# Delta-rule inverse in packed 64x64 blocks, mask applied at the eviction, last level on one quarter

## What is computed

```python
def chunk_gated_delta_rule(q, k, v, g, beta):
    ...
    m = jnp.where(strict, jnp.einsum('bhncd,bhnsd->bhncs', k_beta, k) * decay, 0.0)
    rhs = jnp.concatenate([v_beta, k_beta * jnp.exp(g)[..., None]], axis=-1)
    sol = lax.linalg.triangular_solve(m + jnp.eye(C, dtype=jnp.float32), rhs, left_side=True, lower=True,
                                      unit_diagonal=True)
    u = sol[..., :Dv]
    w = sol[..., Dv:]
    intra = jnp.where(lower_incl, jnp.einsum('bhncd,bhnsd->bhncs', q, k) * decay, 0.0)
```

## Time and profile before

| | us |
|---|---|
| median of three runs | 2671.65 |
| their lowest and highest | 2669.71, 2673.22 |
| the profiled execution | 2668.37 |
| span of the profiled execution (first to last instruction) | 2666.6 |
| mean granted clock of TensorE | 0.992 of 2.4 GHz |
| TensorE busy | 2585.2 |
| loop of layer 0, L1178's first start to L1242's first | 63.1 |
| loop of layer 1, the same | 62.3 |

### The profile page before, as it was taken

One profiled execution on the slowest core, in us unless ns is written; L12 is line 12 of the kernel. 1 busy time (PEld: TensorE's weight loads), 2 busy tenths in 40 slices (PEclk: granted clock), 3 DMA queues, 4 the chain that ended last, 5 costly groups with the idle time before them and its releaser, 6 DMA issues.

```text
span 2666.6 us, 34482 instructions
## 1 busy us (share of the span) xinstructions
PE 2585.2 (97%) x11814; PEld 2057.1 (77%) x11814; DVE 1553.7 (58%) x1973; ACT 1122.2 (42%) x1610; POOL 112.4 (4%) x101
## 2 busy tenths in 40 slices
PE   7999999999999999999989899999899999899998
PEld 5768888887678888876679778888676788688886
DVE  4656755756556736656886554344569775543444
ACT  5554433435554424432565442232424754422323
POOL 1000000000000000000110010000102000100000
PEclk9999999999999999999999999999999999999998
DMA  4203332333113323342210223233222201233332
GB/s 131 72 1 95 95 110 87 100 101 87 33 42 98 108 84 95 104 110 63 57 56 1 64 79 106 85 100 100 66 64 56 64 9 48 71 98 99 95 98 91
DMA packets 394583, 208.01 MB, mean 78 GB/s; under 512 B 9738, under 2 KB 392660, under 8 KB 394484
## 3 DMA queue, kind: packets, MB, share of 16 engines
q1 hardware_dynamic: 391396, 202.79, 26.4%
...
## 4 chain that ended last, share of the span: by engine, by line
PE 89%; DVE 6%; ACT 3%; issue 1%; DMA 0%; SPq 0%; DVEq 0%; ACTq 0%
PE ps L607 64%; PE ps L626 6%; PE ps L884 2%; PE ps L1178 2%; PE ps L1192 1%; DVE ps L2693 1%; DVE x_sb L2696 1%; ACT whi L1402 1%; PE ps L1037 1%; PE ps L1052 1%; PE ps L1204 1%; DVE yc L2432 1%; DVE h_lo L2687 1%; PE ps L939 1%; PE ps L941 1%
## 5 line engine op out<-in xcount | busy, mean ns | idle before, releaser
L1402 ACT ACTIVATE whi<-raw 128x1024 fp32r<-128x1024 f32 (+1 forms) x354 | 395.8, 1119 | 1062.7 <-PE ps L607 946.3
L607 PE MATMUL ps<-h_hi,whi 128*128 128x512 f32 x1984 | 788.3, 397 | 4.6 <-ACT whi L1402 4.0
L607 PE MATMUL ps<-h_lo,whi 128*128 128x512 f32 x1984 | 772.8, 389 | 0.0
L607 PE MATMUL ps<-h_hi,wlo 128*128 128x512 f32 x1984 | 530.3, 389 | 0.0
L2030 DVE TENSOR_TENSOR wlo<-raw,whi 128x1024 fp32r<-128x1024 f32 (+1 forms) x354 | 458.6, 1296 | 55.5 <-ACT whi L1402 54.5
L607 PEld LDWEIGHTS ps<-h_hi,whi 128*128 128x128 f32 x1984 | 372.7, 188 | 89.6 <-ACT whi L1402 8.2
L607 PEld LDWEIGHTS ps<-h_lo,whi 128*128 128x128 f32 x1984 | 372.6, 188 | 82.5 <-issue 6.2
L607 PEld LDWEIGHTS ps<-h_hi,wlo 128*128 128x128 f32 x1984 | 372.4, 188 | 77.4
L607 PE MATMUL ps<-a_hi,whi 128*128 128x512 f32 x592 | 230.3, 389 | 0.0
L607 PE MATMUL ps<-a_lo,whi 128*128 128x512 f32 x592 | 230.3, 389 | 0.0
L2728 DVE TENSOR_TENSOR cv<-ps,rstd 128x512 f32<-128x512 f32 x88 | 60.9, 692 | 248.9 <-PE ps L607 241.0
...
## 6 DMA issues: line engine op xcount, KB each, us to landing
...
```

Of the source, the lines that this page charges most:

```text
L607: return pe.matmul(ps[:, ACC[s], :], w[s][:, k, :], r[:, k, :], start=start, stop=stop)
L1402: act.activation(whi[s][:, 0:kt, :], raw[s][:, 0:kt, :], ACT.Copy).then_inc(w_hi_ready.sem, 1)
```

## The change

Every matrix is 128x128 and, up to the next to last level, block diagonal with two 64x64 blocks. The change keeps only these blocks (`HB` = 64). `xd` and `xdT` (X and its transpose) each hold 4 x 64 columns, partitions 0 to 63 for the upper block and 64 to 127 for the lower, both inside `gk`. A product of one head becomes 8 of 64x64 with 64 columns: for each chunk one that reads and writes partitions 0 to 63, and one that reads and writes 64 to 127 of the same bank. Turning becomes a product with a 64x64 identity. The mask is applied to the first product when VectorE takes it from PSUM (`p1c`), in place of ScalarE's copy and of `lt`; `lev` holds turned masks for that. The second product goes to `ACC`, and the layer norm's sums to `TRN`. The update of n-1 stands in VectorE's iteration n. In steps 16 to 19 it writes the two blocks into `xT`, in two operations; the last level (steps 20 to 23) has 4 products of one quarter, ScalarE copies the first with its sign turned, and VectorE copies the second into the quarter of `xT` that is left. GpSimd zeroes columns 0 to 63 of each matrix of `xT` once per layer, behind head 0. In the heads, q k' comes before k k', turning uses bank `STAT[0]`, and the mask of level 0 is two operations on 64 partitions.

```diff
-        lt, p1, mrs2, msq2 = kb, dm, kb, sqt
+        p1, mrs2, msq2 = dm, kb, sqt
+        p1c = dm[:, 0, :].rearrange("p (a n) -> p a n", a=2)
+        xd, xdT = gk[:, :, 0:TB * HB], gk[:, :, TB * HB:2 * TB * HB]
...
                     delta_head(h)
+                    if h == 0:
+                        nc.gpsimd.memset(xT[:].rearrange("p h (t d) -> p (h t) d", d=P)[:, :, 0:HB], 0.0).then_inc(low_zeroed.sem, 1)
...
                 def head_products(h):
+                    if h >= 1:
+                        pe.wait_ge(intra_made.sem, intra_made.at(L, h - 1))
+                    for tb in range(TB):
+                        mm = pe.matmul(ps[:, STAT[1], tb * P:(tb + 1) * P], gk[:, h, tb * P:(tb + 1) * P],
+                                       gq[:, h, tb * P:(tb + 1) * P], start=True, stop=True)
+                    mm.then_inc(qk_ready.sem, 1)
                     pe.wait_ge(kb_ready.sem, kb_ready.at(L, h))
                     if h >= 1:
-                        pe.wait_ge(intra_made.sem, intra_made.at(L, h - 1))
+                        pe.wait_ge(x0_new.sem, x0_new.at(L, h - 1))
                     for tb in range(TB):
                         mm = pe.matmul(ps[:, STAT[0], tb * P:(tb + 1) * P], gk[:, h, tb * P:(tb + 1) * P],
                                        kb[:, h % 2, tb * P:(tb + 1) * P], start=True, stop=True)
                     mm.then_inc(kk_ready.sem, 1)
-                    if h >= 1:
-                        pe.wait_ge(x0_new.sem, x0_new.at(L, h - 1))
-                    for tb in range(TB):
-                        mm = pe.matmul(ps[:, STAT[1], tb * P:(tb + 1) * P], gk[:, h, tb * P:(tb + 1) * P],
-                                       gq[:, h, tb * P:(tb + 1) * P], start=True, stop=True)
-                    mm.then_inc(qk_ready.sem, 1)
...
                 def head_turned(h):
                     pe.wait_ge(lt0_ready.sem, lt0_ready.at(L, h))
                     for tb in range(TB):
-                        c = slice(tb * P, (tb + 1) * P)
-                        mm = pe.transpose(ps[:, STAT[1], c], xT[:, h, c], ident[:])
+                        for r in range(2):
+                            rows_r, c = block(r, tb, HB)
+                            mm = pe.matmul(ps[rows_r, STAT[0], c], xdT[rows_r, h, c], ident[rows_r, rows_r], start=True, stop=True)
                     mm.then_inc(p0_ready.sem, 1)
...
                 def level_first(n):
                     h = n % GH
-                    pe.wait_ge(lt_ready.sem, lt_ready.at(L, n))
                     if n == 0:
                         pe.wait_ge(eg_ready.sem, eg_ready.at(L, GH - 1))
                     elif n == 1:
                         pe.wait_ge(kb_ready.sem, kb_ready.at(L, GH - 1))
+                    elif n < STEPS - GH + 2:
+                        pe.wait_ge(p1_masked.sem, p1_masked.at(L, n - 2))
                     else:
-                        pe.wait_ge(p1_kept.sem, p1_kept.at(L, n - 2))
-                    if n >= GH:
+                        pe.wait_ge(p1_turned.sem, p1_turned.at(L, n - 2 - (STEPS - GH)))
+                    if n < GH:
+                        pe.wait_ge(x0_new.sem, x0_new.at(L, n))
+                    else:
                         pe.wait_ge(xt_kept.sem, xt_kept.at(L, n - GH))
                     for tb in range(TB):
-                        c = slice(tb * P, (tb + 1) * P)
-                        mm = pe.matmul(ps[:, ROT[n % 2], c], lt[:, n % 2, c], gk[:, h, c], start=True, stop=True)
+                        c = slice(tb * HB, (tb + 1) * HB)
+                        if n < STEPS - GH:
+                            for r in range(2):
+                                rows_r, diag_c = block(r, tb, P)
+                                mm = pe.matmul(ps[rows_r, ROT[n % 2], c], gv[rows_r, h, diag_c], xd[rows_r, h, c], start=True, stop=True)
+                        else:
+                            mm = pe.matmul(ps[HB:P, ROT[n % 2], c], gv[0:HB, h, tb * P + HB:(tb + 1) * P], xd[0:HB, h, c],
+                                           start=True, stop=True)
                     mm.then_inc(p1_ready.sem, 1)
...
                 def level_second(n):
                     h = n % GH
-                    pe.wait_ge(p1_kept.sem, p1_kept.at(L, n))
-                    if n < GH:
-                        pe.wait_ge(x0_new.sem, x0_new.at(L, n))
+                    if n < STEPS - GH:
+                        pe.wait_ge(p1_masked.sem, p1_masked.at(L, n))
+                    else:
+                        pe.wait_ge(p1_turned.sem, p1_turned.at(L, n - (STEPS - GH)))
                     if n >= 2:
                         pe.wait_ge(x_new.sem, x_new.at(L, n - 2))
                     else:
-                        pe.wait_ge(turned_used.sem, turned_used.at(L, GH - 1))
+                        pe.wait_ge(acc_free.sem, V * 2 + N_IN2 + 2)
                     for tb in range(TB):
-                        c = slice(tb * P, (tb + 1) * P)
-                        mm = pe.matmul(ps[:, TRN[n % 2], c], p1[:, n % 2, c], xT[:, h, c], start=True, stop=True)
+                        c = slice(tb * HB, (tb + 1) * HB)
+                        if n < STEPS - GH:
+                            for r in range(2):
+                                rows_r = slice(HB * r, HB * (r + 1))
+                                mm = pe.matmul(ps[rows_r, ACC[n % 2], c], p1c[rows_r, n % 2, c], xdT[rows_r, h, c], start=True, stop=True)
+                        else:
+                            mm = pe.matmul(ps[0:HB, ACC[n % 2], c], p1c[HB:P, n % 2, c], xT[HB:P, h, tb * P + HB:(tb + 1) * P],
+                                           start=True, stop=True)
                     mm.then_inc(xpt_ready.sem, 1)
...
+                        pe.wait_ge(intra_made.sem, intra_made.at(L, GH - 1))
                     for tb in range(TB):
-                        c = slice(tb * P, (tb + 1) * P)
-                        mm = pe.transpose(ps[:, STAT[n % 2], c], xT[:, h, c], ident[:])
+                        c = slice(tb * HB, (tb + 1) * HB)
+                        if n < STEPS - 2 * GH:
+                            for r in range(2):
+                                rows_r = slice(HB * r, HB * (r + 1))
+                                mm = pe.matmul(ps[rows_r, STAT[n % 2], c], xdT[rows_r, h, c], ident[rows_r, rows_r], start=True, stop=True)
...
+                    if n == 2:
                         head_turned(GH - 1)
                     if n == 15:
...
-                    act.wait_ge(p1_ready.sem, p1_ready.at(L, n))
-                    if n >= 2:
+                    if n >= STEPS - GH:
+                        act.wait_ge(p1_ready.sem, p1_ready.at(L, n))
                         act.wait_ge(xpt_ready.sem, xpt_ready.at(L, n - 2))
-                    else:
-                        act.wait_ge(intra_made.sem, intra_made.at(L, GH - 2 + n))
-                    order.told(act.activation(p1[:, n % 2, :], ps[:, ROT[n % 2], :], ACT.Copy), p1_kept, L, n)
+                        order.told(act.activation(p1c[HB:P, n % 2, :], ps[HB:P, ROT[n % 2], 0:TB * HB], ACT.Copy, scale=-1.0),
+                                   p1_turned, L, n - (STEPS - GH))
                     if 0 <= n - 2 < STEPS - GH:
+                        upto = P if n - 2 < STEPS - 2 * GH else HB
                         act.wait_ge(xt_turned.sem, xt_turned.at(L, n - 2))
-                        order.told(act.activation(gk[:, (n - 2) % GH, :], ps[:, STAT[n % 2], :], ACT.Copy), xt_kept, L, n - 2)
+                        order.told(act.activation(xd[0:upto, (n - 2) % GH, :], ps[0:upto, STAT[n % 2], 0:TB * HB], ACT.Copy), xt_kept, L, n - 2)
...
                     dve.wait_ge(turned_used.sem, turned_used.at(L, h))
-                    order.told(dve.tensor_tensor(intraT[:, h, :], ps[:, STAT[1], :], dm[:, s, :], ALU.mult), intra_made, L, h)
-                    order.settle()
-                    order.told(dve.tensor_tensor(by_token(xT[:, h, :]), by_token(gv[:, h, :]),
-                                                 lev[:, 0, :].unsqueeze(1).to_broadcast([P, TB, P]), ALU.mult), lt0_ready, L, h)
+                    order.told(dve.tensor_tensor(gv[:, h, :], ps[:, STAT[0], :], dm[:, s, :], ALU.mult), intra_made, L, h)
+                def head_masked(h):
+                    order.settle()
+                    for r in range(2):
+                        rows_r = slice(HB * r, HB * (r + 1))
+                        ins = dve.tensor_tensor(by_block(xdT[rows_r, h, :]), by_token(gv[rows_r, h, :])[:, :, rows_r],
+                                                lev[rows_r, 0, :].unsqueeze(1).to_broadcast([HB, TB, HB]), ALU.mult)
+                        if r == 0:
+                            order.step(ins)
+                        else:
+                            order.told(ins, lt0_ready, L, h)
...
                     order.settle()
-                    order.step(dve.tensor_tensor(by_token(gk[:, h, :]), unit_blocks, by_token(ps[:, STAT[1], :]), ALU.subtract))
```

(50 more changed lines are left out.)

35 lines of the change are left out of this document (22 added, 13 removed).

## The result

The changed kernel takes 2651.61 us (2649.48 to 2655.48), the kernel before on the same chip 2671.13 (2669.71 to 2673.22): a ratio of 0.9928, with a 95% interval of 0.9911 to 0.9945. The change takes off 19.5 us where I had forecast 33; 2651.6 lies in the range, 13.6 us above the predicted 2638. The profiled execution's span is 2648.6 us, 18.0 less than before, and TensorE's mean granted clock is 0.987 (0.992 before).

What follows compares the result with a forecast made beforehand. TensorE was taken to bound the kernel, with VectorE close behind. Gains of 1.0+3.0+2.3+6.3+4.1 = 16.7 us per layer, 33 for two, gave 2638 us; the range was 2626 to 2662, holding about 0.8.

Steps and rivals of the forecast that it cites:

- The pair of tiles: Two 64x64 matmuls in different array tiles run side by side at 0.058 us a pair, 0.46 us per product.
- the low bound: Pair pace taken from L823's second weight loads starting 0.06 us later, against 0.110 at the other bound; chance 0.60.
- The rule of the Trainium skill: Different row tiles cannot access the same PSUM bank simultaneously; by it the pair of tiles would serialize.
- doesn't go below 0.110: Rival: tiles take turns on the bank or the sequencer limits feeding; products 0.88 us, 2676 us, slower; chance 0.13.
- in between: Rival: feeding costs something, 0.080 us a pair, a step of 1.92, 2653 us; chance 0.18.
- signs of being wrong: A product taking 0.64 us or more, TensorE waiting in plain steps, or granted clock 0.50 beyond the entry.
- The heads: Heads before the loop: shorter VectorE operations and the query product filling a wait; about 1.0 us off per layer.
- The entry: From head 2's turning to the first L1204: 11.0 us instead of 14.06, 3.0 off per layer.
- Steps 3 to 7: Loop steps with a convolution tap, bounded by VectorE: 1.76 us instead of 2.22, 2.3 off per layer.
- The plain steps: Loop steps without a tap, bounded by TensorE: 1.39 us instead of 2.22; steps 8 to 15 give 6.3 off per layer.
- The end: From the first product of step 16 to L1242: 16.9 us instead of 21.0, 4.1 off per layer.
- the clock as a rival: Clock stays at 1.2 GHz through the loop, as small tiles with waits may not count as work; 2695 us; chance 0.06.

Runs made afterwards that it cites:

- late masks: The changed kernel, with GpSimd masking the four intraT only after the update of step 9 instead of behind each head: 2646.92 us, ratio 0.9911.
- All together with the taps: The changed kernel with GpSimd's masks late, taps in steps 4, 6, 8, 10, 12 and 13, and filler matmuls at loop end, heads and entry: 2640.03 us.
- second profile: The changed kernel run again, unedited, to stand beside the edited runs: 2650.72 us, ratio 0.9931.

## Why the forecast was right in sign and half right in size

**The pair of tiles** was right: 0.058 us forecast, 0.0583 measured, granted clock 1.00. The choice of the low bound by the weight loads of L823 held. The rule of the Trainium skill that the prediction names against it has no effect to be seen here: both row tiles write the same bank, on different partitions, and the pair does not serialize; where the page and this measurement differ, the measurement decides. The rival "doesn't go below 0.110" is out, and so is "in between".

**The number is partly luck.** The case that came true, the pair at 0.058, had its own range of 2628 to 2648, and the measured time is 3.6 us above it. It lies in the band given to "in between", 2648 to 2662, whose mechanism did not occur. The stated range held the time because it was wide enough for a rival that is out. One of the prediction's own signs of being wrong also came up: the granted clock was 0.50 beyond the entry, in the first products behind it, at the loop's end and in the right-hand sides. And the product that stands at L1242 came 12.3 us sooner after head 2's turning in layer 0 and 14.0 in layer 1, not some 16.

**The heads** were the first term that failed. I had 1.0 off; in layer 0, head 0's turning to head 2's went from 18.4 us (1368.57 to 1386.96) to 20.9 (1368.55 to 1389.46), 2.5 more. The step was "Splitting the mask in two adds 0.1": it added 1.17 (1.86 for 0.69), because GpSimd's mask runs in between. I had written of GpSimd that nobody needs its zeros before the loop ends, and not asked whether its operations hold up VectorE's. The halved subtractions did shrink by 0.53, as forecast. VectorE also stood 0.37 us longer ahead of them in layer 0 (0.47 for 0.10, in layer 1 not), which no run explains. With that, k k' of head 1 starts 0.86 later than q k' did (1372.69, 1371.83). The other 1.6 us is the clock: from there to the next weights takes 5.2 us against 3.6, at a granted 0.61. Before, the window right behind the wait of 1.76 showed no fall:

```profile
1372.00:1377.00 5.00, 5.00 (x39) 4.74 (x40) 4.79 (x7) 3.05 (x10) 2.98 (x2) 1.00 0.31 108
```

Here it follows a wait of 2.37, and in the run with late masks one of 1.84, so the length of the last wait alone does not decide it.

**The entry** was right in its sum: 10.85 us from head 2's turning to the first turning of a step, 11.2 in layer 1, 11.0 forecast; with the clock at 1.2 GHz for some 3 us, as assumed. But its terms were off and cancelled. Head 3's two masks took 1.82 us beside GpSimd's, where some 0.9 was left for them, and ended 6.0 us after head 2's turning instead of 5.4; what followed, the slow clock included, took 4.9 instead of 5.6.

**Steps 3 to 7** were mis-sized a little: mask to mask is 1.87, not 1.76, and TensorE waits for VectorE in them, as forecast (0.26 us each). In layer 0 the first four products behind the entry ran at half the clock, 0.86 us apart (1400.31 to 1403.75), which the forecast had not; so layer 0 gained 6.9 of 8.6 us up to step 16, layer 1 8.2. The plain steps are 1.40, 1.39 forecast.

**The end** was right in its mechanism: in layer 1, at a granted clock of 1.00, it took 17.2 us, 16.9 forecast. In layer 0 it took 18.9 with the centred sum at half speed (3.61 for 1.98). And in both layers the right-hand sides behind it, which I had left unchanged, lost 2.3 and 1.6 us at 1.2 GHz. I had named the clock as a rival, with 0.06, but with the wrong mechanism: small tiles in the loop. From step 4 on the loop's small tiles ran at 1.00 in both layers. What happened is that a shorter TensorE leaves waits where before there was work, and these can cost twice, once as waits and once in the work behind them.

**Account,** in layer 0 and layer 1, from the first profile: 33.4 forecast for both, 17.7 found. Heads and entry fell short by 3.3 and 4.1 (forecast 4.0, found 0.7 and 0.1 lost), the middle by 1.7 and 0.4, the end by 2.0 and 0.3, and behind it 2.3 and 1.6 were lost: 15.7. The clock's part was measured by filling the waits: 3.9 for the loop's end, 2.2 for the heads and entry in part; the contention's part by the late masks: 3.8. All together with the taps gave 10.7 of the 13.6 us between forecast and time; by the stretches most of the shortfall is found. Between these parts the split is uncertain by the noise named above. What is open is when the clock falls: among executions of one and the same kernel it falls at different places. In the changed kernel's second profile L1277 ran at full speed and the centred sum in 3.67.
